# Filling the expert ring's slots in the work region one by one, and refilling the first gate slots in halves

## The reference, cut to what matters

```python
def hier_moe(h, w_rg, w_re, w_gate, w_up, w_down):
    ...                                  # routing: one group of 4, two experts of 8 in it
    gates = jnp.sum(jax.nn.one_hot(expert_idx, N_EXPERTS, dtype=jnp.float32) * weights[..., None], axis=-2)
    hg = jnp.einsum('nld,edf->nlef', h, w_gate)
    hu = jnp.einsum('nld,edf->nlef', h, w_up)
    act = jax.nn.silu(hg) * hu * gates.astype(h.dtype)[..., None]
    return jnp.einsum('nlef,efd->nld', act, w_down)
```

## Time and profile before

| | us |
|---|---|
| median of 3 runs | 1066.71 |
| lowest and highest | 1065.88, 1069.83 |
| span of the profiled execution | 1069.3 |
| TensorE busy in it | 960.5 (90%) |
| DVE, ACT, POOL busy | 429.5, 237.7, 88.8 |
| expert stage of layer 0, first expert product to last | 393.4 to 611 |
| expert stage of layer 1 | 843.7 to the end |
| DMA over the span | 292.58 MB, mean 274 GB/s |

### The profile page before, as it was taken

One profiled execution on the slowest core, in us unless ns is written; L12 is line 12 of the kernel. 1 busy time (PEld: TensorE's weight loads), 2 busy tenths in 40 slices (PEclk: granted clock), 3 DMA queues, 4 the chain that ended last, 5 costly groups with the idle time before them and its releaser, 6 DMA issues.

```text
span 1069.3 us, 17954 instructions
## 1 busy us (share of the span) xinstructions
PE 960.5 (90%) x6734; PEld 572.3 (54%) x6734; DVE 429.5 (40%) x1107; ACT 237.7 (22%) x513; POOL 88.8 (8%) x199
## 2 busy tenths in 40 slices
PE   8999989899989999977779899999999999777695
PEld 6777767586885365533434344444454755334341
DVE  3733455465854346423533400252002563324343
ACT  3421145354301141110111211231002411001012
POOL 6333241140000000000000000000000000000000
PEclk9999999999999999988999999999999999889899
DMA  9961187794701599999999964433334899999994
GB/s 290 249 174 31 41 255 242 255 349 192 257 2 50 183 407 379 421 420 420 421 420 418 357 227 158 158 141 115 148 119 175 359 423 420 421 420 421 417 416 174
DMA packets 90060, 292.58 MB, mean 274 GB/s; under 512 B 16099, under 2 KB 52507, under 8 KB 62030
## 3 DMA queue, kind: packets, MB, share of 16 engines
q1 hardware_dynamic: 75508, 267.63, 65.2%
q0 software_dynamic: 5152, 17.05, 5.1%
q10 hardware_dynamic: 9306, 6.67, 2.0%
HBM read 286.17 MB, written 5.16 MB: 272 GB/s over the span
## 4 chain that ended last, share of the span: by engine, by line
PE 72%; DMA 16%; DVE 7%; ACT 2%; issue 1%; SPq 1%; ACTq 0%; DVEq 0%
DMA arena<-in_moe_w_up 15%; PE ps L1583 10%; PE ps L886 10%; PE ps L1337 9%; PE ps L1323 4%; PE ps L1673 4%; PE ps L1000 3%; PE ps L810 2%; PE ps L1388 2%; PE ps L1013 2%; PE ps L1089 2%; PE ps L801 2%; PE ps L1354 1%; PE ps L830 1%; PE ps L1576 1%
## 5 line engine op out<-in xcount | busy, mean ns | idle before, releaser
L1337 PE MATMUL ps<-arena,hT 128*32 128x512 f32 x896 | 112.2, 658 | 50.5 <-DMA arena<-in_moe_w_up 49.9
L1583 PE MATMUL ps<-arena,hT 128*128 128x512 f32 x256 | 111.0, 593 | 0.0
L886 PE MATMUL ps<-hT,arena 128*128 128x288 f32 x448 | 110.0, 407 | 0.0
L1323 PE MATMUL ps<-lvl,htok 128*128 128x128 f32 (+1 forms) x768 | 95.5, 281 | 7.9 <-DVE x L2551 7.7
L1337 PEld LDWEIGHTS ps<-arena,hT 128*32 128x32 f32 x896 | 33.6, 120 | 124.3 <-issue 124.3
L1323 PEld LDWEIGHTS ps<-lvl,htok 128*128 128x128 f32 x768 | 90.2, 191 | 15.8 <-issue 10.5
L886 PEld LDWEIGHTS ps<-hT,arena 128*128 128x128 f32 x448 | 84.6, 190 | 23.5 <-issue 0.5
L1583 PEld LDWEIGHTS ps<-arena,hT 128*128 128x128 f32 x256 | 48.3, 190 | 59.7 <-issue 59.4
L1440 PE MATMUL ps<-arena 128*128 128x512 f32 x112 | 55.3, 618 | 4.4 <-DVE x L2545 4.4
L1388 PE MATMUL ps<-arena 128*32 128x512 f32 x448 | 51.0, 595 | 0.0
L2537 DVE TENSOR_SCALAR hT<-ps,nw 128x128 f32<-128x128 f32 (+1 forms) x64 | 22.7, 355 | 68.5 <-PE ps L1323 68.4
(11 more groups left out here) (477 smaller groups left out, 1285.7 us busy)
## 6 DMA issues: line engine op xcount, KB each, us to landing
arena<-in_moe_w_gate SPq DMA_DIRECT2D x64, 1024.0 KB, 20.0
arena<-in_moe_w_up SPq DMA_DIRECT2D x64, 1024.0 KB, 21.8
arena<-in_moe_w_down SPq DMA_DIRECT2D x56, 1024.0 KB, 21.4
arena<-in_cache_k SPq DMA_DIRECT2D x64, 256.0 KB, 4.2
arena<-in_cache_v POOLq DMA_DIRECT2D x64, 256.0 KB, 3.9
arena<-in_w_in_odd SPq DMA_DIRECT2D x16, 1024.0 KB, 11.0
arena<-in_w_in_even SPq DMA_DIRECT2D x14, 1024.0 KB, 9.0
arena<-in_moe_w_down SPq DMA_DIRECT2D x16, 512.0 KB, 15.3
```

Source lines behind the costliest of these rows:

```text
L886: last = mm(ps[:, c % 4, 0:T], w[:, k, P * (c % 2):P * (c % 2 + 1)], hT[:, k, :], start=k == 0, stop=k == KD - 1)
L1323: last = mm(ps[:, row_bank(k), 0:w], htok[:, i, P * k:P * (k + 1)], pl[:, i, 0:w], start=i == 0, stop=i == 2)
L1337: last = mm(ps[EC * j:EC * (j + 1), q % 2, :], xgT[q % 2][:, k, EC * j:EC * (j + 1)], ring[:, sl:sl + 2, DE * k:DE * (k + 1)], start=k == ...
L1583: last = mm(ps[:, bank, :], hT[:, k, P * i:P * (i + 1)], ring[:, oslot(2 * n):oslot(2 * n) + 2, QC * k:QC * (k + 1)], start=k == 0, stop=k ...
```

## The change

Only SP's program changes in order; TensorE gets the semaphores for it.

1. The ten units 8 to 17 no longer wait for the end of the mixer. `fill_even` and `fill_odd` issue each group when the last reader of its slots' memory is done, in between units 0 to 7. In layer 0: units 14 to 17 after `dl_oss_ps` 1 and `dl_vexp` 8, units 10 to 13 after `dl_su` 8, units 8 and 9 after `out_misc` 13. In layer 1: 14 and 15 after `gm_sum` 6, 17 after w_used of slot 3, 16 after `gm_m_ps` 9, 8 to 10 after `out_misc` 14, 11 to 13 after `gm_t_ps` 16, then units 6 and 7.
2. Units 18 to 21, the refills of turn 0's gate slots, go out in two halves of 512 KB each (`refill_half`): columns of k = 0 to 3 when the gate part has done k = 3 (a new count of `part_ps`), the rest when it has done k = 7. The first halves count on `half_loaded` (the former `wd_half`), the second on the slot's semaphore. TensorE waits for both ahead of turn 1.
3. The counts of `part_ps` and `half_loaded` shift accordingly in the other places that use them.

```diff
@@ wait_moe, TensorE
             if isinstance(r, int):
                 wait_first(eng, layer, ("unit", u))
+                if RSLOTS <= u < RSLOTS + QE:
+                    eng.wait_ge(s.half_loaded, 16 * QE * (2 * layer + 1))
@@ first_free, SP
                 if old in [gate_no(0, 0, w) for w in range(QE)]:
-                    sp.wait_ge(s.part_ps, 2 * layer + 1)
+                    sp.wait_ge(s.part_ps, 3 * layer + 2)
@@ SP
+            def refill_half(layer, u, hf):
+                q, j, e = u // MSLOTS, u % MSLOTS, place_of(u)
+                gates = [gate_no(0, q, w) for w in range(QE)]
+                m = WD if j >= 2 * QE else WG if u in gates else WU
+                sl, cs = moe_slot(0, u), slice(UNIT // 2 * hf, UNIT // 2 * (hf + 1))
+                sp.dma_start(ring[:, sl, cs], m[layer, e:e + 1].rearrange("e (p k) f -> p (e k f)", p=P)[:, cs])\
+                    .then_inc(s_w[sl] if hf else s.half_loaded, 16)
+
             def first_loads(layer):
-                for u in range(RSLOTS, MOE_UNITS):
+                sp.wait_ge(s.part_ps, 3 * layer + 1)
+                for u in range(RSLOTS, RSLOTS + QE):
+                    refill_half(layer, u, 0)
+                for u in range(RSLOTS, RSLOTS + QE):
+                    first_free(layer, u)
+                    refill_half(layer, u, 1)
+                for u in range(RSLOTS + QE, MOE_UNITS):
@@ SP, new
+            def fill_even():
+
+                def over_weights(*us):
+                    for u in us:
+                        even_used(EVEN_UNITS - SLOTS + (u - EVEN_UNITS) % SLOTS)
+                        moe_load(0, 0, u)
+
+                over_weights(2, 3, 4, 5)
+                sp.wait_ge(s.dl_oss_ps, 1)
+                sp.wait_ge(s.dl_vexp, NB)
+                for u in (14, 15, 16, 17):
+                    moe_load(0, 0, u)
+                over_weights(6, 7, 0)
+                sp.wait_ge(s.dl_su, 8)
+                for u in (10, 11, 12, 13):
+                    moe_load(0, 0, u)
+                over_weights(1)
+                sp.wait_ge(s.out_misc, 16 * 13)
+                for u in (8, 9):
+                    moe_load(0, 0, u)
...
@@ SP, the two layers
                 if layer == 0:
-                    for u in (2, 3, 4, 5, 6, 7, 0, 1):
-                        even_used(EVEN_UNITS - SLOTS + (u - EVEN_UNITS) % SLOTS)
-                        moe_load(0, 0, u)
+                    fill_even()
                 else:
-                    for u in range(SLOTS):
-                        odd_used(ODD_UNITS - SLOTS + u)
-                        moe_load(1, 0, u)
-                sp.wait_ge(s.x_new, 6 * layer + 3)
-                sp.wait_ge(s.out_misc, 16 * (13 + layer))
-                for u in range(SLOTS, RSLOTS):
-                    moe_load(layer, 0, u)
+                    fill_odd()
                 first_loads(layer)
@@ gate_part, TensorE
+                        if q == 0 and part == 0 and KD // 2 - 1 in ks:
+                            last.then_inc(s.part_ps, 1)
```

More of the change, by code:

```diff
@@ L65 @@
  p_rdy p_chain pw_rdy spb_ps spb_act spb_dve g_ps xgd xga gu_ps silu act t_ps at_ev dn_ps y_ev o_ps xadd
- hot_ps hot_act hot_dve wd_half part_ps
+ hot_ps hot_act hot_dve half_loaded part_ps
  rr_done  out_misc dve_chain act_chain pool_chain """.split()
@@ L512, in down_half @@
                              WD[layer, bass.ds(which, 1)].rearrange("e (p c) d -> p (e c) d", p=P)[:, :, cs])\
-                    .then_inc(s.wd_half if hf else s_w[sl], 16)
+                    .then_inc(s.half_loaded if hf else s_w[sl], 16)
             def first_free(layer, u):
@@ L548, in first_loads, with fill_odd, over_weights @@
                     down_half(layer, u, sp.value_load(perm[0:1, place_of(u):place_of(u) + 1], min_val=0, max_val=NE - 1), 1)
+            def fill_even():
[16 more added lines that the diff above has]
+                    moe_load(0, 0, u)
+            def fill_odd():
+                def over_weights(*us):
+                    for u in us:
+                        odd_used(ODD_UNITS - SLOTS + u)
+                        moe_load(1, 0, u)
+                sp.wait_ge(s.gm_sum, 6)
+                for u in (14, 15):
+                    moe_load(1, 0, u)
+                over_weights(0, 1, 2, 3)
+                moe_load(1, 0, 17)
+                over_weights(4)
+                sp.wait_ge(s.gm_m_ps, HC + 1)
+                moe_load(1, 0, 16)
+                sp.wait_ge(s.out_misc, 16 * 14)
+                for u in (8, 9, 10):
+                    moe_load(1, 0, u)
+                over_weights(5)
+                sp.wait_ge(s.gm_t_ps, NU)
+                for u in (11, 12, 13):
+                    moe_load(1, 0, u)
+                over_weights(6, 7)
             def odd_load(j):
@@ L1394, in down_half @@
                         if hf:
-                            pe.wait_ge(s.wd_half, 16 * QE * (layer + 1))
+                            pe.wait_ge(s.half_loaded, 16 * QE * (2 * layer + 2))
                         else:
@@ L1962, in turn @@
                         if first and q == NQ - 1:
-                            act.wait_ge(s.part_ps, 2 * layer + 2)
+                            act.wait_ge(s.part_ps, 3 * layer + 3)
                         else:
```

## The result

| | median of 20 runs | lowest to highest | profiled execution's span |
|---|---|---|---|
| before | 1069.41 us | 1065.79 to 1072.25 | 1069.3 |
| after | 1072.57 us | 1067.15 to 1075.39 | 1071.1 |

After to before is **1.0022, with a 95% interval of 1.0011 to 1.0032**: the change loses about 2.4 us, inside what the prediction called no change, on the other side of zero from its forecast. The 1060.4 us and the range from 1058.0 to 1066.0 were wrong. (The kernel before itself stands at 1069.41 us over 20 runs, against 1066.71 for the three of the prediction; the ratio doesn't carry that difference.)

The account below looks back on a forecast made before the run. The expert-weight stream was taken to bound both expert stages from turn 3 on. Layer 0 -3.63 + 0.14 + 0.7 = -2.79, layer 1 -3.49, together -6.3 us: from the median 1066.71 to 1060.4 us, range 1058.0 to 1066.0.

Parts of the forecast that it names:

- the routing of layer 0: Serial part begun by DVE's MEMSET, which waits for out_delta_sample; forecast 0.7 us later.
- layer 0's stream: Expert-weight refills of layer 0: 3.63 us gained by the earlier start, 0.14 lost to 4 KB rows.
- layer 1's: Expert-weight refills of layer 1: the same -3.63 + 0.14 = -3.49 us, with no routing delay.
- What bounds the kernel.: Both expert stages: from turn 3 TensorE runs at the weight stream's pace, so an earlier stream start ends them earlier.
- The first half 3.63 us earlier.: First refill in each layer: issued after gate k = 3, at 398.46 instead of 402.09 in layer 0.
- 0.14 us a layer: Refill halves: 4 KB rows at w_out_odd's 417 GB/s instead of 423 lose 0.14 us a layer.
- 0 to 1.45 us, I take 0.7: Layer 0 routing: delay because out_delta_sample shares the DMA with early loads, assuming queues alternate in coarse pieces.
- Rival A: Output goes last behind five loads, landing at 384.6; routing 3.95 us late, 1063.7 us; chance 0.35 including delays of 1.5 to 4.
- By itself it gains nothing: Early fill: no gain alone, but lets the first halves start at once; otherwise 0.5 to 1.5 of 3.63 us lost.
- C: Refill stream: early start not passed on, free slots or SP's queue become the limit; 1066 us; chance 0.10.
- D: Rival A plus loads and stores mixing slowly, 1.4 times the time, out_misc at 393; 1072 us; chance 0.07.
- What would show it.: Trace signs: MEMSET row decides; turn 3's wait about 2.4 us; wrong if turn 7 waits over 1 or layer 1 gains under 3.

Follow-up runs that it names:

- e3_halves: Kernel before plus only the refill of units 18 to 21 in halves, no early fill; 1067.95 us, ratio 0.9978 to before.
- n1_whole_4k: As e4, but each refill of units 18 to 21 is one 1 MB transfer of 256 rows of 4 KB; 1066.58 us, run once.
- m1: Changed kernel, out_delta_sample on its own semaphore, both column halves of each refill issued together after k = 7; 1072.01 us, run once.
- e4: Changed kernel with out_delta_sample on its own semaphore and units 18 to 21 refilled whole; 1069.87 us, ratio 1.0005 to before.
- m5: As e4, but turn 4's four down units go as column halves, issued with 20 us of stream ahead; 1070.10 us, run once.
- e2_freed: Changed kernel whole, with out_delta_sample on its own semaphore so DVE's MEMSET no longer waits for it; 1066.60 us, ratio 0.9978 to before.
- m2_part_late: As m1, but a half is 64 partitions of 8 KB rows instead of half the columns; 1091.4 us, run once.
- e1_whole: Changed kernel with its early fill, but units 18 to 21 refilled whole at k = 7; 1073.67 us, ratio 1.0039 to before.
- v3_order: Changed kernel, but SP waits for the 13 output transfers before issuing units 10 to 13; 1069.41 us, ratio 1.0006 to before.

## Why the prediction was wrong, point by point

In the profiles the forecast of -6.3 us missed + 2.5 us by three terms: the routing of layer 0 (+ 0.7 forecast, + 3.73 measured), layer 0's stream (- 3.49, - 0.39) and layer 1's (- 3.49, - 0.83). The second and third, 5.8 us together, are the larger part. Slow halves account for 3.5 of the 5.8, counted in bytes; for the rest, between the stream and TensorE, no run names the cause.

**What bounds the kernel.** Right in the main, though a stream ahead by 1.5 and 2.1 us brought turn 7 forward by only 0.39 and 0.83. The stream and its start set the end: e3_halves moves nothing but that start, and gains.

**The first half 3.63 us earlier.** Right in size: 3.73 us between the two issues in layer 0 of after, 3.74 in layer 1.

**"0.14 us a layer" for the 4 KB rows.** The term that failed most. Counted in bytes it measured 2.2 us in layer 0 and 1.6 in layer 1, 11 to 16 times as much; and by turn 7 only 0.39 and 0.83 us of the 3.73 had reached TensorE. The nearest row was read for the wrong property. The row of w_out_odd has 4 KB rows, but its transfers hold 1 MB. By n1_whole_4k the price of the rows themselves is 0.3 us, near the 0.14; that of halving the transfers, with a thinly filled queue, was never bounded, though the edit does both. The kernel before has such transfers itself: the last turn's down units go as eight of 512 KB, in rows of 2 KB, issued by L511 from 573.25 to 591.4 and landing 9.6 to 19.2 us later. Window of the kernel before:
```profile
590.00:595.00 5.00, 4.71 (x39) 1.67 (x42) 1.74 (x3) 0.00 (x0) 0.00 (x0) 1.00 1.04 384
```
At 384 GB/s instead of 420 the 4.2 MB of four units in halves take 0.9 us more, an estimate from this row. It would have put 0.9 a layer in place of 0.14, still under half of what layer 0 lost. The Trainium skill, in "DMA: Bandwidth & Descriptors", section "Bandwidth", tells to make each DMA 1 MiB or more to reach 75% of the peak. It speaks against the edit and was not weighed either. The traces agree with its direction at the start of a stream (361 GB/s in m1 against 393 in e4), but its figure is not borne out: there 512 KB came to 316 of 417 GB/s, already 76%, and in the deep queue of m5 to 408.

**"0 to 1.45 us, I take 0.7" for the output.** Rival A had the order right: five loads first, then the output. A's bounds need correcting on two points. With the 0.73 us between the two profiles added, the last byte moved at about 382.4, where A had 382.6, and the output was seen at 383.1 instead of 384.6: its tail from last byte to semaphore was 0.7 us, not 2.0. So the routing started 2.47 us late and not 3.95. Against that, A counted the wait alone; the 1.57 us of lowered clock stood in no case. The two errors nearly cancel, which is luck: A's price was 3.95, the measured one 3.73. The choice between forecast and A leant on one row of 4 KB pieces. The rule of the Trainium skill, in "DMA: Bandwidth & Descriptors", section "Queues, rings and completion order" (each DMA engine takes turns between the queues packet by packet), makes a turn of small rows worth few bytes, and the trace agrees: 5.2 of the first 5.4 MB were the loads'. It should have decided here, as nothing in the trace spoke against it for rows of 512 B.

**"By itself it gains nothing", the early fill clears the way.** The first half is right (e4, 1.0005). The second was worth nothing that can be measured: e3_halves, where the first halves stand behind the ten loads, has the same 0.9978 as e2_freed.

**Rivals C and D.** C put the kernel level with before, near what came, but for another reason: no wait for free slots shows in the stream (DMA share 1.01 over 430:560 in after), but the bytes were slow. D gave 1072 us, the number that came, by luck: its 1072 was 5.3 us over a base of 1066.71, and the base itself stands at 1069.41. Its mechanism, a mix at 1.4 times the time, didn't occur (`out_misc` came at 382.3, not 393). The losing side had a price, but the wrong one: A plus slow halves is what happened, two terms that no case had put together.

**What would show it.** The MEMSET row decided for A, as said. Turn 3's wait of 2.4 us didn't come (5.72), turn 7 of layer 1 waits more than 1 us, and layer 1 gained 0.83 where under 3 was to count as wrong.

## What to carry to other kernels

When an edit splits a transfer, look for rows that match it in size, row length and depth of the queue alike; one that matches in row length alone priced this edit at less than a tenth. Before loads are moved earlier, list the outputs that share the DMA in that stretch and whose semaphore the routing or any other serial part counts: here one shared count turned a free transfer into 3.7 us, and a semaphore of its own gave it back. Price a new wait of TensorE together with the lowered clock that can follow it, 1.6 us here behind a wait of 2.

No kernel measured is clearly better than e2_freed and e3_halves, both 0.22% faster than before (0.05 to 0.39%, and 0.05 to 0.38%); e3_halves is the smaller edit.

## What the runs showed of the hardware

- Transfers that write 64 of the 128 partitions ran at 230 GB/s with the engines fully busy, where those over 128 partitions ran at about 420 (m2_part_late).
- Transfers of 512 KB in 4 KB rows: 267 to 361 GB/s over 10 us near the start of a stream, 320 for 3 us behind some whole units, 408 in a deep queue. The 1 MB transfers of the same row length ran at 385 in the second microsecond and 414 in the third (n1_whole_4k). Transfers of 512 KB in 2 KB rows at the end of a stream: 384 (before).
- A 2.1 MB output in 512 B rows gave way to 5.2 MB of loads in 8 KB rows until these were through, and was seen 21.1 us after its issue (after).
- TensorE's clock fell to 0.50 some 2.6 us after the end of a 1.99 us wait, with the engine busy since, and stayed low for about 3.4 us (after); the same behind a wait of 2.07 us (e1_whole). Without the wait it stayed at 1.00 (before, v3_order).
